# Attention with two shared PSUM banks and scores issued first, and filter sums taken as rows in four column groups

## What is computed

```python
def hyena_filter(L, w1, b1, freq, w2, b2, w3, decay):
    ...
    h = h * jnp.exp(-offset[:, None] * jnp.abs(f32(decay))[None, :])
    return h / (jnp.sum(jnp.abs(h), axis=0, keepdims=True) + EPS)

def block_attention(q, k, v):          # 8 heads of 64, 2 key/value heads, blocks of 128 queries
    ...
        s = jnp.einsum('bqkgd,bskd->bkgqs', qblk, k) * scale
        p = jax.nn.softmax(s, axis=-1).astype(v.dtype)
        return jnp.einsum('bkgqs,bskd->bqkgd', p, v)
```

## Time and profile before

| | |
|---|---|
| median of 3 runs | 4371.22 us (4369.33 to 4372.78) |
| the profiled execution | 4360.98 us, its span 4359.0 us |
| PE busy | 3926.4 us, 90% of the span |
| PEld busy | 3152.1 us, 72% |
| DVE busy | 1756.0 us, 40% |
| ACT busy | 1102.8 us, 25% |
| granted PE clock, mean | 0.955 |

### The profile page before, as it was taken

One profiled execution on the slowest core, in us unless ns is written; L12 is line 12 of the kernel. 1 busy time (PEld: TensorE's weight loads), 2 busy tenths in 40 slices (PEclk: granted clock), 3 DMA queues, 4 the chain that ended last, 5 costly groups with the idle time before them and its releaser, 6 DMA issues. The chain is left out here.

```text
span 4359.0 us, 55904 instructions
## 1 busy us (share of the span) xinstructions
PE 3926.4 (90%) x23853; PEld 3152.1 (72%) x23853; DVE 1756.0 (40%) x2865; ACT 1102.8 (25%) x2095; POOL 184.5 (4%) x203
## 2 busy tenths in 40 slices
PE   7999979998499999997999999999687399999995
PEld 4544545553299999996888888888543399999995
DVE  3325457733611111111377887888832511111112
ACT  3110135422011110111354455454422001011111
POOL 1000000000000000000000000000000000000000
PEclk8999999999699999999999999999898699999998
DMA  5311010024978888885101001100224388888884
GB/s 182 106 72 70 16 49 1 1 73 153 312 238 258 264 258 264 256 259 155 41 27 33 28 29 30 32 17 19 98 78 145 115 255 257 263 258 259 257 260 158
DMA packets 515926, 615.14 MB, mean 141 GB/s; under 512 B 16474, under 2 KB 466700, under 8 KB 512992
## 3 DMA queue, kind: packets, MB, share of 16 engines
q1 hardware_dynamic: 492480, 525.18, 37.3%
q0 software_dynamic: 19872, 75.69, 6.3%
q10 hardware_dynamic: 3328, 10.71, 0.6%
HBM read 558.36 MB, written 53.17 MB: 140 GB/s over the span
## 5 line engine op out<-in xcount | busy, mean ns | idle before, releaser
L1671 PEld LDWEIGHTS moe_pgu<-step_hnT,mw_w 128*128 128x128 f32 x8192 | 1117.3, 191 | 16.5 <-issue 16.5
L1671 PE MATMUL moe_pgu<-step_hnT,mw_w 128*128 128x160 f32 x8192 | 1125.0, 300 | 3.4 <-ACT step_hnT L1711 3.4
L1735 DVE TENSOR_TENSOR moe_hT<-moe_sg,moe_pgu 128x160 f32<-128x160 f32 x256 | 82.1, 321 | 1027.4 <-PE moe_pgu L1671 972.0
L1683 PE MATMUL moe_pol<-mw_w,moe_hT 128*128 128x256 f32 x2048 | 457.5, 381 | 2.3 <-DVE moe_hT L1735 1.0
L1922 PE MATMUL rec_pz<-step_hnT,rec_w 128*128 128x256 f32 x1920 | 424.5, 380 | 3.5 <-ACT l_zc L1994 1.9
L1683 PEld LDWEIGHTS moe_pol<-mw_w,moe_hT 128*128 128x128 f32 x2048 | 383.2, 190 | 59.0 <-DVE moe_hT L1735 9.9
L1722 ACT ACTIVATE moe_sg<-moe_pgu 128x160 f32<-128x160 f32 x256 | 77.6, 303 | 1317.8 <-PE moe_pgu L1671 1317.8
L1922 PEld LDWEIGHTS rec_pz<-step_hnT,rec_w 128*128 128x128 f32 x1920 | 362.7, 191 | 52.0 <-ACT l_zc L1994 2.3
L1926 PE MATMUL rec_pz<-rec_w,step_hnT 128*128 128x256 f32 x1280 | 288.1, 384 | 15.1 <-ACT rec_zg L1997 15.1
L1926 PEld LDWEIGHTS rec_pz<-rec_w,step_hnT 128*128 128x128 f32 x1280 | 243.9, 193 | 50.6 <-ACT rec_zg L1997 17.9
L1952 PE MATMUL rec_pg<-rec_ring 128*128 128x128 f32 x1600 | 196.5, 281 | 47.1 <-DVE rec_AT L2249 19.7
(11 more groups left out here) (367 smaller groups left out, 4414.8 us busy)
## 6 DMA issues: line engine op xcount, KB each, us to landing
mw_w<-in_moe_w_gu SPq DMA_DIRECT2D x256, 1024.0 KB, 10.6
mw_w<-in_moe_w_down SPq DMA_DIRECT2D x128, 1024.0 KB, 13.0
mw_w<-in_mod_w SPq DMA_DIRECT2D x24, 1024.0 KB, 14.3
rec_w<-in_r_w_in SPq DMA_DIRECT2D x40, 512.0 KB, 4.0
late_w<-in_mod_w POOLq DMA_DIRECT2D x16, 1024.0 KB, 6.7
scratch_xm<-op_x ACTq DMA_DIRECT2D x20, 512.0 KB, 2.6
scratch_xn<-op_xn POOLq DMA_DIRECT2D x20, 512.0 KB, 5.4
mod_w<-in_mod_w SPq DMA_DIRECT2D x8, 1024.0 KB, 16.5
```

The lines of the kernel that those rows point to most:

```text
L1671: m = nc.tensor.matmul(pgu[2 * (f % 2) + part][:, :], w[:, j, k, (f % 2) * P:(f % 2 + 1) * P], ring[:, k, e % 8, :], start=(k == 0), stop= ...
L1683: m = nc.tensor.matmul(pol[q // 2][:, (q % 2) * SW:(q % 2 + 1) * SW], hT[:, k, 0:CL], w[:, 8 + q, k, :], start=(k == 0), stop=(k == KD - 1))
L1735: nc.vector.tensor_tensor(hT[:, f, :], sg[:, f % 2, :], pgu[2 * (f % 2) + 1][:, :], ALU.mult).then_inc(multiplied, 1)
```

## The change

It has two parts.

**Filter sums.** The ten tiles become the moving operand (512 columns) and `ones` the weight of one column. Tile n of a sequence goes to column group n % 4, so that partial sums of the sequence arrive as rows 0, 32, 64 and 96 of one bank (`psl[c]`). DVE zeroes both banks before (in its list ahead of the filter's products), copies both to `part` afterwards, and eight products of a 128x128 block of `part` with `ones` add the rows and turn them into the columns that `pss` held before.

**Attention.** `t_ps` and `o_ps` give way to two banks `to_ps`, which the list `uses` deals out in turn to the transposes of a group ("t") and the products of a pair ("o"); a use waits for the use two before it to be copied out. PE's list for pair i is now: scores of pair i+1, groups 0 to 3, all 20 products of pair i-1, group 4. DVE's maximum is one reduction over all blocks, which waits for all chunks, and `output(i-1)` stands ahead of the copy of group 4.

```diff
+        part = room[:, 6:8, :].rearrange("p k t -> p (k t)")[:, 0:2 * HW].rearrange("p (c n) -> p c n", c=2)
...
             pe.wait_ge(abs_ready, NT)
+            pe.wait_ge(part_zero, 1)
             for c, (o, ln) in enumerate(SEQS):
+                nt = ln // P
+                for n in range(nt):
+                    q = 32 * (n % 4)
+                    m = nc.tensor.matmul(psl[c][q:q + 1, :], ones[:, :], win[:, o // P + n, :], start=(n < 4), stop=(n >= nt - 4),
+                                         tile_position=(0, q))
+            m.then_inc(parted, 1)
+            pe.wait_ge(part_out, 2)
+            for c in range(2):
                 for ch in range(4):
-                    for t in range(o // P, (o + ln) // P):
-                        m = nc.tensor.matmul(pss[:, 4 * c + ch:4 * c + ch + 1], win[:, t, ch * P:(ch + 1) * P], ones[:, :],
-                                             start=(t == o // P), stop=((t + 1) * P == o + ln))
+                    m = nc.tensor.matmul(pss[:, 4 * c + ch:4 * c + ch + 1], part[:, c, ch * P:(ch + 1) * P], ones[:, :], start=True, stop=True)
...
             layer(1)
+            dve.wait_ge(arg_ready, 2)
+            for c in range(2):
+                r = nc.vector.memset(psl[c][:, :], 0.0)
+            r.then_inc(part_zero, 1)
...
+            dve.wait_ge(parted, 1)
+            for c in range(2):
+                nc.vector.tensor_copy(part[:, c, :], psl[c][:, :]).then_inc(part_out, 1)
             dve.wait_ge(summed, 1)
...
+    uses = []
+    for i in range(N):
+        late = len(groups[i]) - 1
+        uses += [("t", i, g) for g in range(max(1, late))] + ([("o", i - 1, 0)] if i else []) + ([("t", i, late)] if late else [])
+    uses.append(("o", N - 1, 0))
+    at = {use: n for n, use in enumerate(uses)}
...
-        t_ps = ps("t_ps", [P, 512])
-        o_ps = ps("o_ps", [P, 512])
+        to_ps = [ps(f"to_ps{i}", [P, 512]) for i in range(2)]
...
+            def bank_free(*use):
+
+                if at[use] >= 2:
+                    kind, i, g = uses[at[use] - 2]
+                    if kind == "t":
+                        copied(pe, gfirst[i] + g + 1)
+                    else:
+                        pe.wait_ge(o_out, i + 1)
...
             for i in range(N):
-                ng = len(groups[i])
-                for g in range(ng):
+                late = len(groups[i]) - 1
+                if i + 1 < N:
+                    for j in range(len(chunks[i + 1])):
+                        scores(i + 1, j)
+                for g in range(max(1, late)):
                     transposes(i, g)
-                    if g == 0 and i + 1 < N:
-                        for j in range(len(chunks[i + 1])):
-                            scores(i + 1, j)
-                    if i and (g or ng == 1):
...
-                            products(i - 1, a0, a1)
-            products(N - 1, 0, pairs[N - 1][3])
+                if i:
+                    products(i - 1)
+                if late:
+                    transposes(i, late)
+            products(N - 1)
...
                 for r in range(2):
                     x = 2 * i + r
+                    dve.wait_ge(qk, 2 * first[i + 1] + r - 1)
+                    nc.vector.tensor_reduce(nmax[:, x:x + 1], s_ps[:, r, 0:nk * P], AX_X, ALU.max, negate=True).then_inc(maxed, 1)
...
                 copy(i, 3)
                 if i + 1 < N:
                     normalise(i + 1, 0)
+                if i:
+                    output(i - 1)
                 copy(i, 4)
                 if i + 1 < N:
                     normalise(i + 1, 1)
-                if i:
-                    output(i - 1)
```

More of the change, by code:

```diff
@@ L1141, in _, with bank @@
             next_loads(sp)
+        def bank(*use):
+            return to_ps[at[use] % 2]
         def copied(eng, n):
@@ L1165, in transposes, with products @@
                 pe.wait_ge(normed, 2 * i + 1 + max(r for r, _ in group))
-                copied(pe, gfirst[i] + g)
+                bank_free("t", i, g)
                 for n, (r, a) in enumerate(group):
-                    m = nc.tensor.transpose(t_ps[:, n * P:(n + 1) * P], p[:, i % 2, r, a * P:(a + 1) * P], S["ident"][:, :])
+                    m = nc.tensor.transpose(bank("t", i, g)[:, n * P:(n + 1) * P], p[:, i % 2, r, a * P:(a + 1) * P], S["ident"][:, :])
                 m.then_inc(tr, 1)
-            def products(i, a0, a1):
+            def products(i):
                 pr, t, k0, nk = pairs[i]
-                if a0 == 0:
-                    copied(pe, gfirst[i + 1])
-                    if i:
-                        pe.wait_ge(o_out, i)
-                for a in range(a0, a1):
+                copied(pe, gfirst[i + 1])
+                bank_free("o", i, 0)
+                for a in range(nk):
                     for r in range(2):
-                        m = nc.tensor.matmul(o_ps[64 * r:64 * r + HD, 0:P], v[:, k0 + a, (pr // 2) * HD:(pr // 2 + 1) * HD],
+                        m = nc.tensor.matmul(bank("o", i, 0)[64 * r:64 * r + HD, 0:P], v[:, k0 + a, (pr // 2) * HD:(pr // 2 + 1) * HD],
                                              pT[:, i % 2, r * nk + a, :], start=(a == 0), stop=(a == nk - 1))
-                if a1 == nk:
-                    m.then_inc(pv, 1)
+                m.then_inc(pv, 1)
             for j in range(len(chunks[0])):
@@ L1220, in _ @@
                     nc.scalar.activation(pT[:, i % 2, 4 * g:4 * g + len(group), :].rearrange("p a c -> p (a c)"),
-                                         t_ps[:, 0:len(group) * P], ACT.Copy).then_inc(act_out, 1)
+                                         bank("t", i, g)[:, 0:len(group) * P], ACT.Copy).then_inc(act_out, 1)
                 if i + 1 < N:
@@ L1230, in maxes @@
                 nk = pairs[i][3]
-                parts = [(0, 8), (8, nk - 8)] if nk > 8 else [(0, nk)]
                 for r in range(2):
                     x = 2 * i + r
[L1234 to L1242, removed]
+                    dve.wait_ge(qk, 2 * first[i + 1] + r - 1)
+                    nc.vector.tensor_reduce(nmax[:, x:x + 1], s_ps[:, r, 0:nk * P], AX_X, ALU.max, negate=True).then_inc(maxed, 1)
             def normalise(i, r):
@@ L1255, in copy @@
                 dve.wait_ge(tr, gfirst[i] + g + 1)
-                nc.vector.tensor_copy(pT[:, i % 2, 4 * g:4 * g + 4, :].rearrange("p a c -> p (a c)"), t_ps[:, :]).then_inc(dve_out, 1)
+                nc.vector.tensor_copy(pT[:, i % 2, 4 * g:4 * g + 4, :].rearrange("p a c -> p (a c)"), bank("t", i, g)[:, :]).then_inc(dve_out, 1)
             def output(i):
@@ L1260, in output @@
                 dve.wait_ge(pv, i + 1)
-                nc.vector.tensor_copy(yT[:, pr, t * P:(t + 1) * P], o_ps[:, 0:P]).then_inc(o_out, 1)
+                nc.vector.tensor_copy(yT[:, pr, t * P:(t + 1) * P], bank("o", i, 0)[:, 0:P]).then_inc(o_out, 1)
             maxes(0)
```

10 lines of the change are left out of this document (2 added, 8 removed).

## The result

The changed kernel takes 4332.75 us (median of four runs, 4329.28 to 4337.05) against 4370.27 us of the kernel before: the ratio is 0.9914, with a 95% interval of 0.9897 to 0.9931. A second comparison, on another occasion with six and seventeen runs, gave 0.9926 (0.9914 to 0.9939). So the change is worth 32 to 38 us, and the forecast was 4335.

A forecast was written before the change was run, and what follows sets the result against it. PE was taken as the bound in latent pairs, by its work and waits for a single transpose bank. Attention's 28 us plus startup's 8 gave 36: 4371.2 - 36 = 4335 us, range 4329 to 4347 (0.75).

The forecast's parts named there:

- The bound: Attention's latent pairs: PE's own work of 7.96 us plus 0.89 waiting on a single transpose bank make 8.85 us.
- The pair: Attention, latent pair in rhythm: 8.85 us becomes 8.05, 0.80 less, over 28 steps 22.4 us.
- Grouping as the source of the gain: Latent pair: six changes of kind fewer cut PE's own work from 7.96 to 7.16 us.
- two banks hardly buy waiting time: Latent pair: PE's waits stay 0.89 us with two banks, as much as before.
- The head: Attention's first latent pairs, with no transposes to hide the chain maximum to exponential: about 3 us saved (1 to 4).
- the tail: Attention after the last scores: loses one group's waits, 0.8 us saved.
- the context pairs: Attention's context pairs: 3.51 us become 3.2 each; seven pairs save 2 us.
- Startup: End of `startup`: ten row products, copies and 16 column records replace 80 records; 8.1 us saved.
- The sum: Whole kernel: attention 28 us (18 to 34) plus startup 8, together 36 us less.
- The scores did not become the wait: Rival, latent pair: late exponentials hold up the scores, whose cover is 0.18 us; 4345 at 0.3 beyond; chance 0.12.
- The rows did run side by side: Rival, `startup`: sums do not run side by side, or the clock falls early; 7 us less gain, 4342; chance 0.05.
- Transposes did not drop the clock: Rival, latent pairs: clock at 0.50 in every pair, 12.9 us against 8.85, 4490 in all; chance 0.03.

The follow-up runs named there:

- products cut in two: The changed kernel with a pair's products split into ten on either side of group 4; 4337.14 us in one run, 8.39 us a latent pair.
- rows in one group: The changed kernel with all row products of a sequence in column group 0, added up there; the ten products take 8.74 us, `hin_pst` starts at 58.34.
- products behind group 2: The changed kernel with the previous pair's products after group 2 instead of group 3, and the output copied earlier; 4325.66 us, ratio 0.9896.

## Why the prediction was right, and where it was not

**The bound.** Right: PE, in work and in waits for the bank. The other engines have room: ACT waits 3.66 us ahead of its first copy of a pair, and in `startup` the row products took the place of the 80 records that ended the stage.

**The pair, from 8.05 to 8.23.** The mis-sized term. Laid out 0.80 us less, measured 0.62; over the 28 steps in rhythm 17.0 us instead of 22.4. The largest part, 0.15, is the hand-over from ACT's third copy to the products: the layout started them 0.10 behind the copy (5.04 to 5.14), as transposes do, and they start 0.25 behind it. Up to the end of that copy the layout is 0.02 short (ACT's first copy 0.06 late, its third start 0.03 quicker behind group 2), the products are 0.02 shorter than laid out and group 4 is 0.03 longer.

**Grouping as the source of the gain.** Right (one change more costs 0.15, in the products cut in two; PE's own work fell by 0.72 of the 0.80 laid out), but the sentence that two banks hardly buy waiting time hid that the order needs them: with one bank each a pair takes 10.0 us.

**The head, the tail, the context pairs.** The first latent pairs brought 2.2 us instead of 3, the tail behind the last scores 0.4 instead of 0.8, the context pairs 0.7 instead of 2. The context term failed by the clock: 3.92 us a pair at 0.50, and 3.10 where the clock was up, against 3.2 laid out. I had taken for granted that the clock rises where it rose before. Attention came to 20.4 us in the profile and not 28, inside my bounds of 18 to 34, but at their low end.

**Startup.** Right: 7.8 of 8.1 us, row products 2.74 (2.6), columns 1.95 at a clock still at 1.00 (1.8), the two memsets (1.02 us) inside DVE's wait. That `hyena_in` shifts as a whole is not quite so: 1.0 us was given back between `hin_pst` and attention, 0.7 with the sums alone.

**The sum.** Right, and in part by luck. I forecast 36 us. By the profiles the two parts are worth 28 us, by the runs 32 to 38, so terms that were 8 us too large in the profile met a gain in the runs that no term of mine explains. The two profiles of the kernel before (4360.98 and 4357.71 us) lie below its median near 4370, at a mean granted clock of 0.955 against 0.950 in most of the timed runs (two timed runs at 0.955 took 4357.57 and 4358.67 us); those of the changed kernel lie 3 to 9 below its medians, with 0.954. So a part of what the runs show is not in the profiles. I noted that the profiled execution was 10 us under the median and then took the difference as if both had the same offset; which stretches carry the lower clock in the timed runs stays open, since they have no traces.

**The rivals.** The scores did not become the wait: cover 0.5 us, measured. The rows did run side by side. Transposes did not drop the clock: the pairs' stretch of transposes (697.83 to 700.4) lies in a window at 1.00. The Trainium skill (TensorE: Matmul & The Clock Gate, Part 4: PE-mode transpose) would have them not count as busy; that did no harm here, where scores and products stand on either side, and no run of this case puts the rule to the test.

## What to carry to other kernels

Count the changes between kinds of matmul work on PE (here 0.12 to 0.15 us each) as work. Read the hand-over from a copy to PE for each kind of work by itself (here 0.10 us to transposes and 0.25 to products). An order that groups transposes needs a second bank, so that one fills while the other drains (1.8 us a pair here); choose which use takes which bank by whose copy is done first: moving the products one group ahead was worth another 12 us by the medians, 10 of attention in the profiles. When a stage starts elsewhere in time, look again at what granted clock it gets, before reading its length as the effect of an edit.

## What the hardware showed

- The same attention code, starting at 583.1 to 583.5 us and at 575.5 us, found the clock back at 1.00 after 11 us in the one case and after more than 35 in the other, and took 322.9 and 333.0 us. The first has two profiles, the second one. In the new order the time at which the stage begins does not sort the cases: at 575.8 and 575.9 (two profiles of the changed kernel), 582.1 (rows in one group) and 582.4 (products behind group 2) the context pairs ran at 0.50 throughout, at 584.5 (attention alone) the clock was back after 21 us. What decides it I did not settle.
- The clock in `startup` does vary: in the profile of the kernel with the products behind group 2, whose `startup` is the changed kernel's, it was 0.61 on average between 40 and 50 us, where the changed kernel had 1.00, and `hin_pst` started at 58.8 instead of 52.4.

```profile
40.00:50.00 10.00, 9.73 (x38) 2.17 (x36) 2.33 (x5) 4.50 (x9) 0.00 (x0) 0.61 1.06 377
```

So the two profiled spans differ by 3.1 us only (4323.9 and 4327.0), while attention itself is 10.1 us shorter (292.4 and 302.5): single profiles compare stages, not kernels.
